# Retention outputs copied out of their bank by ScalarE, transposes of the gated rows in four banks

## What is computed

```python
qc, kc, vc = (x.reshape(B, H, N, C, 64) for x in (q, k, v))     # H = 8 heads, N = 4 chunks of C = 128
scores = einsum('bhncd,bhnjd->bhncj', qc, kc) * dmask
o_intra = einsum('bhncj,bhnjv->bhncv', scores, vc)
kv = einsum('bhncd,bhncv->nbhdv', kc * zeta, vc)
R[n] = R[n-1] * g_chunk + kv[n-1]
o = o_intra + einsum('bhncd,nbhdv->bhncv', qc, R) * xi
o_ret = rms_norm(o) * silu(rg)                                   # over the 64 columns of a head
mix = concatenate([o_ret, o_diff]) * group_scale
x = x + mix @ w_out
```

## Time and profile before

| | us |
|---|---|
| median of three runs (lowest, highest) | 1597.08 (1595.77, 1597.5) |
| the profiled execution: its own time | 1597.81 |
| its span in the trace | 1595.6 |
| TensorE matmul busy | 1548.2 |
| VectorE, ScalarE, GpSimd busy | 1013.3, 818.2, 206.3 |

### The profile page before, as it was taken

The page is one execution under the profiler, slowest core; times in us unless marked ns, Lnnn a source line. Parts: engine busy times, 40 slices in busy tenths (PEclk is TensorE's granted clock), DMA queues, the critical chain, the costliest instruction groups (busy, mean ns, idle before and its releaser), DMA issues.

```text
span 1595.6 us, 19961 instructions
## 1 busy us (share of the span) xinstructions
PE 1548.2 (97%) x7856; PEld 1249.9 (78%) x7856; DVE 1013.3 (64%) x1689; ACT 818.2 (51%) x1429; POOL 206.3 (13%) x276
## 2 busy tenths in 40 slices
PE   9999999999999999999999999999999999999999
PEld 8877677778877888888777766878767988888887
DVE  4267967765479998999786886555755333334331
ACT  5278776544456888888763435224324333333220
POOL 1000015422234000000252101101001000000000
PEclk9999999999999999999999999999999999999999
DMA  6122121114548999999841112112212232223232
GB/s 238 55 79 80 54 80 54 54 54 148 211 159 238 380 421 421 423 421 421 296 161 62 54 53 80 53 53 66 67 52 80 80 106 94 91 93 107 79 107 92
DMA packets 78640, 235.87 MB, mean 148 GB/s; under 512 B 6961, under 2 KB 9425, under 8 KB 66257
## 3 DMA queue, kind: packets, MB, share of 16 engines
q1 hardware_dynamic: 68288, 207.62, 36.2%
q10 hardware_dynamic: 6624, 14.88, 2.5%
q0 software_dynamic: 3632, 12.08, 2.0%
HBM read 221.97 MB, written 12.60 MB: 147 GB/s over the span
## 4 chain that ended last, share of the span: by engine, by line
PE 80%; DVE 11%; ACT 4%; DMA 2%; issue 1%; POOL 1%; SPq 0%; DVEq 0%; ACTq 0%; POOLq 0%
PE bank L108 76%; PE bank L111 4%; DVE low L133 2%; DVE REST L123 2%; ACT REST L114 2%; DVE REST L133 1%; DVE REST L136 1%; ACT CHH L117 1%; ACT REST L117 1%; DMA slot<-in_w_in 1%; DVE R L123 1%; DVE REST L142 1%; DVE low L123 1%; DVE REST L129 1%; DVE st L139 1%
## 5 line engine op out<-in xcount | busy, mean ns | idle before, releaser
L123 DVE TENSOR_TENSOR low<-slot,CHH 128x1024 fp32r<-128x1024 f32 (+1 forms) x300 | 296.5, 1031 | 117.2 <-ACT CHH L117 116.2
L117 ACT ACTIVATE CHH<-slot 128x1024 fp32r<-128x1024 f32 (+1 forms) x300 | 259.1, 901 | 132.0 <-PE bank L108 55.5
L133 DVE SCALAR_TENSOR_TENSOR low<-slot,smalls,CHH 128x512 fp32r<-128x512 f32 (+1 forms) x232 | 170.5, 765 | 191.2 <-ACT CHH L117 187.2
L108 PE MATMUL bank<-AH,CHH 128*128 128x512 f32 (+1 forms) x640 | 248.2, 388 | 0.2 <-DVE AL L123 0.2
L108 PE MATMUL bank<-AL,CHH 128*128 128x512 f32 (+1 forms) x640 | 242.8, 379 | 0.0
L108 PE MATMUL bank<-AH,low 128*128 128x512 f32 (+1 forms) x640 | 242.6, 379 | 0.0
L117 ACT ACTIVATE CHH<-slot,smalls 128x512 fp32r<-128x512 f32 (+1 forms) x232 | 154.6, 701 | 136.8 <-PE bank L108 67.0
L108 PE MATMUL bank<-CHH,AH 128*128 128x512 f32 x512 | 216.7, 423 | 4.0 <-ACT REST L117 2.8
L108 PE MATMUL bank<-low,AH 128*128 128x512 f32 x512 | 201.2, 393 | 0.0
L108 PE MATMUL bank<-CHH,AL 128*128 128x512 f32 x512 | 200.7, 392 | 0.0
L108 PE MATMUL bank<-CHH,XTF 128*128 128x512 f32 x512 | 161.2, 396 | 1.9 <-DVE REST L120 1.0
(11 more groups left out here) (183 smaller groups left out, 2385.1 us busy)
## 6 DMA issues: line engine op xcount, KB each, us to landing
slot<-in_w_in SPq DMA_DIRECT2D x35, 1024.0 KB, 5.1
slot<-in_w_exp_gate SPq DMA_DIRECT2D x32, 1024.0 KB, 14.3
slot<-in_w_exp_up SPq DMA_DIRECT2D x32, 1024.0 KB, 14.0
slot<-in_w_exp_down SPq DMA_DIRECT2D x32, 1024.0 KB, 14.5
slot<-in_w_gate SPq DMA_DIRECT2D x10, 1024.0 KB, 5.0
slot<-in_w_up SPq DMA_DIRECT2D x10, 1024.0 KB, 5.1
slot<-in_w_down SPq DMA_DIRECT2D x10, 1024.0 KB, 5.1
slot<-in_w_out SPq DMA_DIRECT2D x8, 1024.0 KB, 6.3
```

The costliest lines, as they stand in the source:

```text
L108: return self.e.matmul(out, l, r, start=start, stop=stop) if self.e else Issued()
L117: return self.e.activation(out, in_, ACT.Copy, scale=scale) if self.e else Issued()
L123: return self.e.tensor_tensor(out, a, b, op) if self.e else Issued()
L133: return self.e.scalar_tensor_tensor(out=out, in0=a, scalar=s, in1=b, op0=op0, op1=op1) if self.e else Issued()
```

## The change

For each pair ScalarE now first copies the outputs out of bank 7 into `wk_mem[p]`, which frees the bank, then squares the copy into `rot` (a 128x512 scratch). `rsq` comes from this second instruction, which also waits for the copy itself and for the sum of the pair before (`rsum(p-1)`, which read `rot`). VectorE sums from `rot`, and `rnn` reads the copy in SBUF in place of the bank. The transposes `ry` take a new group of banks, 4, 5, 6 and 7 for p = 0, 1, 2, 3.

```diff
-    banks = Banks(psum, {... "tp": (6,), "op": (7,), ... "row": (3,), "all": tuple(range(8))})
+    banks = Banks(psum, {... "tp": (6,), "op": (7,), ... "row": (3,), "ry": (4, 5, 6, 7), "all": tuple(range(8))})
...
-            b, old = banks.use("tp", ("ry", p))
+            b, old = banks.use("ry", ("ry", p))
...
-            act.activation(wk_mem[p], banks.ap(("ro", p)), ACT.Square).then_inc(*mark("act_rt", ("rsq", p)))
+            act.copy(wk_mem[p], banks.ap(("ro", p))).then_inc(*mark("act_rt", ("rcp", p), ("free", ("ro", p))))
+            act.wait_ge(*at(("rcp", p)))
+            act.wait_ge(*at(("rsum", p - 1) if p else None))
+            act.activation(rot, wk_mem[p], ACT.Square).then_inc(*mark("act_rt", ("rsq", p)))
...
-            dve.reduce(ss, sq.rearrange("p (a v) -> p a v", v=64), ALU.add).then_inc(*mark("dve_rt", ("rsum", p)))
+            dve.reduce(ss, rot.rearrange("p (a v) -> p a v", v=64), ALU.add).then_inc(*mark("dve_rt", ("rsum", p)))
...
-            o = banks.ap(("ro", p))
...
-            dve.tt(sq.rearrange("p (a v) -> p a v", v=64), o.rearrange("p (a v) -> p a v", v=64),
-                   ss.unsqueeze(2).to_broadcast([P, 8, 64]), ALU.mult).then_inc(*mark("dve_rt", ("rnn", p), ("free", ("ro", p))))
+            dve.tt(sq.rearrange("p (a v) -> p a v", v=64), sq.rearrange("p (a v) -> p a v", v=64),
+                   ss.unsqueeze(2).to_broadcast([P, 8, 64]), ALU.mult).then_inc(*mark("dve_rt", ("rnn", p)))
```

More of the change, by code:

```diff
@@ L408, in _build @@
     psum = [ctx.enter_context(nc.psum_tensor(f"bank{i}", [P, 512], F32))[:, :] for i in range(8)]
-    banks = Banks(psum, {"main": (0, 1, 2, 3), "zp": (4, 5), "sb": (4, 5, 6), "tp": (6,), "op": (7,), "four": (0, 1, 2, 3), "three": (0, 1, 2), "gates": (6, 7, 0, 1), "n1": (4, 5, 6, 7), "row": (3,), "all": tuple(range(8))})
+    banks = Banks(psum, {"main": (0, 1, 2, 3), "zp": (4, 5), "sb": (4, 5, 6), "tp": (6,), "op": (7,), "four": (0, 1, 2, 3), "three": (0, 1, 2), "gates": (6, 7, 0, 1), "n1": (4, 5, 6, 7), "row": (3,), "ry": (4, 5, 6, 7), "all": tuple(range(8))})
     rings = []
```

## The result

The changed kernel takes 1592.37 us in the median of 22 runs (1589.89 to 1595.31), the kernel before 1596.4 us in 22 (1591.38 to 1597.97). The ratio is 0.9979, with a 95% interval from 0.9972 to 0.9985: 3.4 us faster by the ratio, 4.0 us by the medians. The forecast was 1592.5 us, 4.6 us faster. The median lies under 1593.9 us, the forecast's bound for faster; by the ratio the gain is 0.21%, and its interval reaches down to 0.15%.

What follows compares the result with a forecast made beforehand. TensorE, busy 97% of the span, bounds the kernel. Removing two waits and a clock fall gives it 5.2 + 1.8 = 7.0 us, but VectorE's queue limits this to 4.6: from 1597.08 to 1592.5 us, range 1589.8 to 1596.0.

Steps and rivals of the forecast that it cites:

- The first wait: TensorE's 1.66 us wait before `ro(3)` in retention, held by `rnn(2)` queued behind a chunk; it goes entirely.
- The number: Forecast time 1592.5 us, 4.6 us under the median 1597.08 of the kernel before; chance 0.64.
- The clock's 3.3 us: TensorE loses 3.3 us to the lower clock behind the wait before `ro(3)`; without the wait the clock stays full.
- The added copy: On ScalarE, copy then square from SBUF adds 0.65 us per pair; hidden for pairs 0 to 2, on pair 3's path.
- `rnn` from SBUF at nothing: On VectorE, `rnn` reading the copy in SBUF instead of the bank costs nothing (bounds 0.06 us either way).
- The four banks: Each `ry(p)` waits for `rn(p)` alone, so TensorE's second wait, 1.78 us before `ry(3)`, goes.
- The rival by the bank rule: VectorE does not hold TensorE back, so all 7.0 us come: 1590.1 us; chance 0.10.
- VectorE next: VectorE's fourth addition sets step 52, 4.6 us earlier; TensorE gets new waits at steps 50 and 52, some 2.4 us.
- one or two falls: Clock falls in the new waits: 3.3 us lost, 1595.8 us, chance 0.15; a second fall later: 1599.1 us, chance 0.06.
- the first wait changes hands: `rw(3)` or another operand still holds `ro(3)` to 1035.5 us; only 0.2 us won, 1596.9 us; chance 0.05.

Runs made afterwards that it cites:

- early `rnn`: Kernel before with the transposes in four banks and `rnn(2)` one step earlier on VectorE, no copy; ratio to before 0.9968.
- filler: Kernel before with 8 more matmuls of 512 columns into a free bank ahead of `ro(3)`, result unused; ratio to before 1.0003.
- three more: Kernel before, unchanged, profiled three more times; start of `ro(2)` to start of step 52 took 30.02, 30.16 and 33.01 us.
- banks alone: Kernel before with the transposes `ry` in four banks and no copy; ratio to before 1.0000.
- wait put back: Changed kernel with each `ro(p)` on TensorE waiting again for the pair before's `rnn`; ratio to before 0.9999.
- late splits: Changed kernel with VectorE's four splits of the gated rows six steps later, behind the additions into R; ratio to before 0.9970.

## Why the prediction was right

*The first wait.* Right. It goes entirely; `rw(3)` ends at 1030.80 + 1.41 = 1032.2 us, in time as forecast. The early `rnn` shows the reason given for it, the place behind the chunk.

*The number.* It is 0.1 us off, and in part by luck: three runs put the kernel before at 1597.08 us, 0.7 us above the median of 22, and the gain is 4.0 us and not 4.6, so two errors cancel.

*The clock's 3.3 us.* This is the step of the sum that was mis-sized. I took the fall of one profile for a fixed part of the kernel before. In six profiles with the wait and no filler (before and its three more, banks alone, wait put back) it fell in four, twice for some 7 us and twice for half of that; in seven without the wait or with it down to 0.2 us it never fell there. A says what a whole fall costs step 52: about 2.6 us, behind the longer wait that goes with it. The mean loss to the clock shows 1.3 to 2.4 us over the kernel, 1.6 us over all runs. The gain of the schedule was 1.7 us by A where the wait had been short (30.02 to 28.36), some 2.2 us where it had been 1.66 us, and 1.2 to 1.6 us by B; the whole 4.8 us came only in executions of the kind that I had read. The measured 3.4 us lie between.

*The added copy, 0.65 us on pair 3's path.* Right: `rsum(3)` 2.9 us earlier, and 0.63 us more with a second copy. For pairs 0 to 2 it is hidden: from the start of `ro(0)` to that of `ro(2)` it takes 20.54 us before and 20.55 after. The earlier trace rows show ScalarE's idle time for pairs 2 and 3 alone; in the same trace it is 2.91 and 2.90 us for pairs 0 and 1.

*`rnn` from SBUF at nothing.* Right: 0.69 us against 0.68. The 62 cycles less that the Trainium skill gives VectorE for a source in SBUF (VectorE: DVE Perf Modes, the section on the TRN2 errata) do not appear in this pair of rows.

*The four banks.* Right in kind: the wait before `ry(3)` goes and returns as waits for VectorE. The rival by the bank rule, all of 7.0 us, is refuted: 1.85 us of TensorE's waits stand before step 52, and the late splits, which touch no bank, take them away.

*VectorE next, step 52 4.6 us earlier.* 4.8 us, with `mix(0)` at 1041.92 + 0.44 = 1042.36 (1042.46 forecast). The two waits sum to 1.85 and not 2.4 us; they are at steps 50 and 52, as forecast.

*The other rivals.* The clock did not fall in the new waits in any profile, so one or two falls there did not come. That the first wait changes hands did not come either.

## What to carry to other kernels

One profile is one execution. Where a clock that falls and a transfer that lands now sooner, now later make up a good part of a gain, read several profiles before the gain is put down as fixed. An instruction that frees a buffer should not stand in its engine's queue behind one that waits for a transfer: moving it one place took away nearly all of the wait (0.22 us were left of 1.1 to 1.7), without the copy's 0.65 us. When the wait for a buffer is taken away, the releasing engine's queue can be the next limit, as VectorE's was here, and what is not needed yet should leave that queue.

## What the runs showed of the hardware

A fall of the clock from 2.4 to 1.2 GHz followed a wait of 1.42 us or more before `ro(3)` (four of four) and none of 1.14 or 1.28 us; but waits of 1.75 to 1.83 us before `ry(3)`, some 15 to 17 us after the start of `ro(3)`, were followed by none (six of six). In cross attention the same wait of 2.82 or 2.83 us went with a fall in 11 of the 14 profiles and with none in three: the late splits, the wait put back and one profile of the kernel before:

TensorE's timeline and the window around it in that profile:

```profile
1157.53 1.96 PE L108 MATMUL bank<-REST 128*128 128x512 f32 x4 [2.82 <-DVE OL L123]
```

```profile
1155.00:1160.00 5.00, 2.48 (x8) 1.42 (x9) 1.79 (x3) 1.60 (x3) 0.00 (x0) 1.00 0.49 190
```

The length of a wait does not decide it alone; what does was not tried. The same transfer of 1 MB, issued at the same place with no other transfer of weights under way, landed 5.06 to 6.57 us after its issue in seven profiles. The whole fall of the earlier trace rows took 0.42 x 2 + 0.50 x 4 + 0.28 x 2 = 3.4 us (the clock is 0.72 from 1042 to 1044 us), so the spread of the kernel before, 1591.4 to 1600.8 us over all its runs, is of the size of two or three falls; that falls make it up is not shown.
